# One of two row blocks of the spare experts' second matrix: three products of high and low parts in place of a native one

## The reference, cut to what matters

```python
def hier_moe(h, wgc, bgc, wgf, bgf, w1, w3, w2):
    ...
    a = jnp.einsum('td,edf->tef', t, w1)
    c = jnp.einsum('td,edf->tef', t, w3)
    act = jax.nn.silu(a) * c * gates[:, :, None].astype(t.dtype)
    y = jnp.einsum('tef,efd->td', act, w2)
    return y.reshape(B, S, D)
```

## Time and profile before

| | |
|---|---|
| median of 3 runs | 2781.2 us (2779.99 to 2784.97) |
| the profiled execution: its time | 2780.18 us |
| its span, first to last instruction | 2778.4 us |
| mean granted TensorE clock | 0.986 of full speed |
| busy share of the span: PE, DVE, ACT, POOL | 98%, 63%, 40%, 58% |
| native products of w2 (L2352) | 368 records, 184 products, 167.3 us busy |
| low parts of expert weights (L3071) | 184, 213.7 us busy, 1218 ns each |

### The profile page before, as it was taken

One profiled execution on the slowest core, in us unless ns is written; L12 is line 12 of the kernel. 1 busy time (PEld: TensorE's weight loads), 2 busy tenths in 40 slices (PEclk: granted clock), 3 DMA queues, 4 the chain that ended last, 5 costly groups with the idle time before them and its releaser, 6 DMA issues. The chain is left out here.

```text
span 2778.4 us, 35448 instructions
## 1 busy us (share of the span) xinstructions
PE 2714.0 (98%) x12442; PEld 2120.3 (76%) x12442; DVE 1741.6 (63%) x2544; ACT 1098.2 (40%) x1899; POOL 1598.2 (58%) x987
## 2 busy tenths in 40 slices
PE   8999999999999999999999999999999999999998
PEld 6777778888887777778888877778776677787775
DVE  6787755444127877654442139777777587777775
ACT  3744323222025544332221031544555415545554
POOL 5754466666677644486666765576236554772253
PEclk9999999999999999999999979999999999999999
DMA  4221222333332322223333322226796132257962
GB/s 154 84 76 61 61 84 84 98 93 96 99 86 86 94 61 61 61 84 99 97 93 97 107 76 87 70 93 237 292 356 212 68 98 69 92 206 268 353 194 65
DMA packets 88762, 337.16 MB, mean 121 GB/s; under 512 B 21296, under 2 KB 24112, under 8 KB 79280
## 3 DMA queue, kind: packets, MB, share of 16 engines
q1 hardware_dynamic: 66592, 298.02, 32.1%
q0 software_dynamic: 19008, 26.28, 3.7%
q10 hardware_dynamic: 3024, 11.01, 1.0%
HBM read 366.67 MB, written 33.55 MB: 144 GB/s over the span
## 5 line engine op out<-in xcount | busy, mean ns | idle before, releaser
L182 POOL TENSOR_TENSOR wl<-ring,wh 128x1024 fp32r<-128x1024 f32 x319 | 783.8, 2457 | 26.6
L180 POOL TENSOR_SCALAR wh<-ring 128x1024 fp32r<-128x1024 f32 x319 | 349.4, 1095 | 742.9 <-PE ps L259 521.9
L257 PE MATMUL ps<-xh,wh 128*128 128x512 f32 x1608 | 639.0, 397 | 14.1 <-DVE xl L1245 10.7
L259 PE MATMUL ps<-xh,wl 128*128 128x512 f32 x1608 | 627.3, 390 | 0.0
L258 PE MATMUL ps<-xl,wh 128*128 128x512 f32 x1608 | 627.1, 390 | 0.0
L257 PEld LDWEIGHTS ps<-xh,wh 128*128 128x128 f32 x1608 | 302.4, 188 | 94.6 <-issue 12.6
L259 PEld LDWEIGHTS ps<-xh,wl 128*128 128x128 f32 x1608 | 302.4, 188 | 64.4
L258 PEld LDWEIGHTS ps<-xl,wh 128*128 128x128 f32 x1608 | 302.7, 188 | 61.6 <-issue 1.0
L1487 DVE SCALAR_TENSOR_TENSOR taps<-ps,par,taps 128x511 f32<-128x511 f32 x192 | 143.9, 749 | 232.9 <-ACT taps L1219 218.1
L3071 DVE TENSOR_TENSOR ew_l<-ew,ew_h 128x1024 fp32r<-128x1024 f32 x184 | 213.7, 1218 | 3.2 <-ACT ew_h L2596 3.2
L2596 ACT ACTIVATE ew_h<-ew 128x1024 fp32r<-128x1024 f32 x184 | 180.3, 1051 | 9.9 <-DMA ew<-in_eu 6.6
(11 more groups left out here) (547 smaller groups left out, 5343.7 us busy)
## 6 DMA issues: line engine op xcount, KB each, us to landing
ring<-in_w SPq DMA_DIRECT2D x343, 512.0 KB, 3.6
ew<-in_eu SPq DMA_DIRECT2D x32, 2048.0 KB, 11.7
ew<-in_ed SPq DMA_DIRECT2D x32, 1024.0 KB, 10.9
xrows<-xr ACTq DMA_DIRECT2D x8, 512.0 KB, 2.7
yrows<-xr ACTq DMA_DIRECT2D x8, 512.0 KB, 3.6
yg<-yrows SPq DMA_DIRECT2D x8, 512.0 KB, 5.1
z<-in_x SPq DMA_DIRECT2D x4, 512.0 KB, 5.7
out<-z SPq DMA_DIRECT2D x8, 256.0 KB, 2.9
```

Source lines behind the costliest of these rows:

```text
L180: nc.gpsimd.tensor_scalar(hi, raw, 1.0, 0.0, ALU.mult, ALU.add).then_inc(sem["w_hi"], 1)
L182: nc.gpsimd.tensor_tensor(lo, raw, hi, ALU.subtract).then_inc(sem["w_split"], 1)
L257: nc.tensor.matmul(out, wh, xh, start=first, stop=False, **kw)
L259: return nc.tensor.matmul(out, wl, xh, start=False, stop=last, **kw)
```

## The change

For tiles 16 to 22 the row block f = 0 of w2 is cut in high and low parts. ACT makes the high part (`down_high`: `dn_h`, 1024 columns, two buffers) at the end of its turn j; it now waits there for the w2 load, which PE waited for before. DVE makes the low part (`down_low`: in place, through `ew_l`) at the end of its turn j, and PE waits for it (`d_lo`). `hidden_evac` of these tiles makes three operations of 128 columns in place of one of 256: the high part `hT_h`, a wait for it, the low part `hT_l`, and the copy of the second block to `hactT`. In `expert_down` of these tiles the f = 0 product of each half becomes three fp32r products; f = 1 stays native. Tiles 0 to 15 are as before.

```diff
@@ expert_down, PE
                         else:
-                            k = j - EXPERTS
-                            pe.wait_ge(sem[f"es_dn{k % 2}"], at(f"es_dn{k % 2}", 16 * (k // 2 + 1)))
+                            pe.wait_ge(sem["d_lo"], at("d_lo", j - EXPERTS + 1))
...
                                 a_ = EW_UP + f * D + half * S
+                                if j >= EXPERTS and f == 0:
+                                    three(nc, ps[:, 5 + half, :], hT_h[:, :], hT_l[:, :], dn_h[j % 2][:, half * S:half * S + S],
+                                          ew_l[:, b, a_:a_ + S], True, False)
+                                    continue
@@ ACT
+                    def down_high(j):
+
+                        k = j - EXPERTS
+                        act.wait_ge(sem[f"es_dn{k % 2}"], at(f"es_dn{k % 2}", 16 * (k // 2 + 1)))
+                        act.wait_ge(sem["dn_mm"], at("dn_mm", j - 1))
+                        if k == 0:
+                            act.wait_ge(sem["hact"], at("hact", j))
+                        A(dn_h[j % 2][:, :], ew[:, j % EW_BUFS, EW_UP:EW_UP + D], ACT.Copy).then_inc(sem["d_hi"], 1)
...
                             weights_high(j + 1, (UP_PARTS - 1,))
+                        if j >= EXPERTS:
+                            down_high(j)
@@ DVE
+                    def down_low(j):
+
+                        dve.wait_ge(sem["d_hi"], at("d_hi", j - EXPERTS + 1))
+                        part = ew[:, j % EW_BUFS, EW_UP:EW_UP + D]
+                        V.tensor_tensor(ew_l[:, j % EW_BUFS, EW_UP:EW_UP + D], part, dn_h[j % 2][:, :], ALU.subtract).then_inc(sem["d_lo"], 1)
+
                     def hidden_evac(j):
 
                         dve.wait_ge(sem["hactt_mm"], at("hactt_mm", j + 1))
+                        if j >= EXPERTS:
+                            do(V.tensor_scalar(hT_h[:, :], ps[:, 4, 0:P], 1.0, None, ALU.mult))
+                            V.tensor_tensor(hT_l[:, :], ps[:, 4, 0:P], hT_h[:, :], ALU.subtract)
+                            V.tensor_copy(hactT[:, 1, :], ps[:, 4, P:2 * P]).then_inc(sem["hactt"], 1)
+                            return
...
                             weights_low(j + 1, (UP_PARTS - 1,))
+                        if j >= EXPERTS:
+                            down_low(j)
```

More of the change, by code:

```diff
@@ L1571 @@
         "e_hi": UP_PARTS * TILES, "e_lo": UP_PARTS * TILES, "silu": TILES,
-        "hact": TILES, "hactt_mm": TILES, "hactt": TILES, "dn_half": TILES, "dn_mm": TILES, "y_lo": TILES, "y_hi": TILES, "y_high": 2,
+        "hact": TILES, "hactt_mm": TILES, "hactt": TILES, "dn_half": TILES, "dn_mm": TILES, "y_lo": TILES, "y_hi": TILES, "d_hi": TILES - EXPERTS, "d_lo": TILES - EXPERTS, "y_high": 2,
         "zt_mm": 4, "zt_taken": 4, "tk_mean": 4, "tk_sq": 4, "tk_std": 4, "tk_rstd": 4, "tk_norm": 3, "tk_last": 1, "xt_mm": 8, "pg_sig": C8, "pp_done": C8, "pt_hi": 4, "pt_lo": 5,
@@ L1637, in second_block @@
         last_l = at_("last_l", 176, [P, D], F32R)
+        dn_h = [at_(f"dn_h{n}", kb, [P, D], F32R) for n, kb in enumerate((172, 184))]
+        hT_h = at_("hT_h", 155, [P, P], F32R)
+        hT_l = at_("hT_l", 155.5, [P, P], F32R)
         sil = at_("sil", 152, [P, DE])
@@ L1682, in second_block @@
                  "ew_up0", "ew_up1", "ew_up2", "ew_dn0", "ew_dn1", "ew_dn2", "es_ua0", "es_ub0", "es_ua1", "es_ub1", "es_dn0", "es_dn1", "e_hi", "e_lo", "up_mm", "silu", "hact", "hactt_mm", "hactt",
-                 "dn_half", "dn_mm", "y_lo", "y_hi", "y_high", "y_out0", "y_out1", "yg_in0", "yg_in1", "yg_in2", "yg_in3", "zt_mm", "zt_taken",
+                 "dn_half", "dn_mm", "d_hi", "d_lo", "y_lo", "y_hi", "y_high", "y_out0", "y_out1", "yg_in0", "yg_in1", "yg_in2", "yg_in3", "zt_mm", "zt_taken",
                  "tk_mean", "tk_sq", "tk_std", "tk_rstd", "tk_norm", "tk_last", "xt_mm", "pg_sig", "pp_done", "pt_hi", "pt_lo", "pq_mm", "pq_evac", "stored", "in_rstd", "in_rows", "consts"])
```

## The result

The changed kernel takes 2789.0 us at the median of 16 runs (2786.2 to 2792.9), beside 2781.2 for the kernel before; the ratio of the runs is 1.0024 with a 95% interval of 1.0017 to 1.0031. Seven later runs of it, beside 29 of the kernel before, gave 1.0029 (1.0018 to 1.0041). It is slower, by a quarter of a per cent. The forecast was 2786.8 in a range of 2783.0 to 2791.5.

A forecast was written before the change was run, and what follows sets the result against it. TensorE bounds the kernel before; VectorE was to bound the changed loop. Spare tiles 5.2 plus end 0.4 give +5.6 us: 2785.8 from the profiled 2780.2, stated as 2786.8 since the median is 1.0 higher; range 2783.0 to 2791.5.

The forecast's parts named there:

- the loop: Spare tiles, through TensorE and VectorE: native products, bank copy, subtractions, hidden copy; period 10.53 us against 10.02 before.
- near 0.9: TensorE's forecast stall ahead of each down product in the spare tiles, in us, with VectorE bounding the loop.
- TensorE's saving: Down products of 14 spare tiles: fp32r in place of native, 0.36 us less a tile, TensorE's own period 9.66.
- Switching between product types: Fp32r to native in down products: taken as 0; rival of up to 0.31 us a switch, +14.3, chance 0.08.
- ScalarE and the load: ScalarE's added 0.97 us copy has 0.7 to spare, and the w2 load is early enough; both cost 0.
- The rival of no overlap: VectorE operations strictly one after another: +1.7 us more, +7.3 in all, 2788.5; chance 0.07.
- a rule against this: VectorE: the next operation waits until the pipe is empty, so both overlaps of 0.08 us would be lost.
- Which tiles pay: Tiles 16 to 20 pay 0.51 us each, tile 21 +0.04; 2.6 a layer, 5.2 for two.
- The end: Tile 22's products end 1.17 us later, 0.7 covered; 0.4 taken for the second layer, 0 for the first.
- the first pick: End of the second layer: 0.5 us of delay left there; 0.4 taken since a later pick waits for its load.
- the addition and the load that were weighed: End of the first layer: last tile's addition and yg load 0.64 us apart, later picks wait for loads; cost 0.

The follow-up runs named there:

- c_neither: Changed kernel without the w2 subtraction and without the low part of the hidden tile (high parts used instead); period of spare tiles 9.70 us.
- d_native: Changed kernel with its ScalarE and VectorE work kept, but native down products on TensorE (f = 1 multiplied twice); period 10.88 us.
- f_earlier_and_order: Changed kernel with both cuts of w2 made earlier in the turn and down products starting with native block f = 1; period 9.66, ratio to before 0.9992.
- n_semaphores_only: Kernel before with only the change's two semaphores declared; ratio to before 1.0003.
- g_order_alone: Changed kernel with down products starting with native block f = 1 and its copy, subtraction of w2 not moved; period 10.02 to 10.04, ratio to before 1.0005.
- before_again: The kernel before, unchanged, run once more for its trace; ratio 1.0002.

## Why the prediction was right

**What bounds the kernel and the loop.** Right. The loop through native products, bank copy, subtractions and hidden copy was forecast at 10.53 and is 10.55. Its terms: five subtractions and the bank copy 6.28 from start to hidden copy (6.28 forecast), hidden copy 0.81 (0.82), from its end to the next bank copy 3.46 (3.43). TensorE's waits of 0.83 by the weight load answer to "near 0.9".

**TensorE's saving.** 0.36 a tile forecast; 3.10 against 3.44 for the down products, c_neither at 9.70 against 10.02 and d_native at +0.33 give 0.32 to 0.34, and f_earlier_and_order at 9.66 the whole 0.36. Switching between product types costs nothing that shows, as taken.

**ScalarE and the load.** Cost nothing, as forecast: in c_neither they are there and the period is 9.70, in f_earlier_and_order 9.66.

**VectorE.** The subtraction is worth 1.14 of VectorE's time in the loop and brings the period from 9.98 to 10.55; the dependent low part of the hidden tile brings it from 10.23 to 10.55. The rival of no overlap would have made the period 10.69. The trace has both overlaps: 2713.50, 2714.63 and 2715.76 are 1.13 apart with a length of 1.22, and the third step of the hidden copy starts 0.21 behind the second (2719.49, 2719.70), which is 0.29 long. The section "The DRAIN you can't avoid" of the Trainium skill's page "VectorE: DVE Perf Modes", which the prediction takes for a rule against this, itself adds that a next operation that is not held starts earlier; the advice on few operations stands in the page's section "Rules for kernel authors".

**Which tiles pay.** Tiles 16 to 20 as forecast. Tile 21 +0.07 where +0.04 was forecast. Sum in the tiles 5.5, forecast 5.2.

**The end.** In the changed kernel the first pick did wait for TensorE, and the third for its load, as forecast (timeline, second layer):

```profile
2773.28 1.22 DVE L3189 SCALAR_TENSOR_TENSOR yg<-yg,ps 128x1024 f32<-128x1024 f32 x1 [0.83 <-PE ps L2379]
...
2776.86 1.22 DVE L3189 SCALAR_TENSOR_TENSOR yg<-yg,ps 128x1024 f32<-128x1024 f32 x1 [0.35 <-DMA yg<-yrows]
```

From tile 21's bank copy to the end are 26.0 and 25.7 us, before 25.3 and 25.7: the 0.4 is not out of line, but can't be told from chance. In the first layer the forecast took 0, and there it was wrong: from tile 21's bank copy to the closing transposes both traces of the changed kernel took 1.3 to 2.1 us more than the three traces of before and n_semaphores_only. What differs there is not the addition and the load that were weighed, but the scatter of tile 21, 1.6 to 1.7 us longer.

**The size.** The medians say +7.9 (the ratio of 1.0024 says 6.7), the forecast +5.6. The tiles bring 5.5 of it, so what is missing lies outside them. The end of the first layer, which the forecast put at nothing, accounts for 1.3 to 2.1 in both traces. Drops of the granted clock come and go between executions of one kernel, and whether the changed kernel meets more of them stays open; so does chance, since a ratio of 1.0020, the forecast's, is inside both intervals. That the total came out in the range is owed to the loop, which was worked out rightly and makes up most of it, and to a range wide enough for a term that was left out.

## What to carry to other kernels

A busy share of 63% says little of an engine's room: VectorE had 0.48 us left on the one stretch that counted, between the copy that releases the bank and the copy that TensorE waits for. Add up the loop through both engines before giving work to the idle one, and put new work where that engine waits for a third one; the same subtraction cost 0.57 us a tile behind the bank copy (2714.63 in the rows above) and nothing some 5 us sooner in the turn, right behind the hidden copy. Where an operand is cut in parts, start with the product that needs no cut: in g_order_alone this alone brought the period from 10.55 to 10.03.

## What was not expected of the hardware

The same small transfer took 2.69 us in one kernel and 4.37 in the other, though its own instruction is the same: the scatter of tile 21 in the first layer took longer in just those nine traces in which a packet of the profile's instruction queue fell into it. If the packet is the cause, which no run here shows, a change can cost time in a place that it doesn't touch.

The clock at the closing transposes differs between executions of one kernel: 5.38 us in before (granted clock 0.69) and 3.93 in before_again (1.00), at the same place in the first layer. A faster TensorE that waits longer may lose a part of its gain there, as f_earlier_and_order did in the last layer (5.38 against 4.01 in before), but one trace does not tell this from chance.
